# Attention pairs: where v is transposed and rounded, and where q is evacuated

## Chip, cores and metric

The kernel runs on one core of one Trainium2 chip. The metric is device time in microseconds of that core, the median over runs. The numbers are float32; products are made from operands split into a rounded high part and a low remainder (hi·hi + lo·hi + hi·lo), three matmuls for one.

## What is computed

A two-layer encoder trunk on x of 512 tokens by 1024 channels. Layer 0 mixes tokens with a Conformer convolution module, layer 1 with forgetting attention (16 heads of 64, causal, 128-query blocks); each is followed by a squared-ReLU MLP. Only the attention bears on the change:

```python
proj = h @ w_in                       # q, k, v for 16 heads, and the forget logits
F = cumsum(log_sigmoid(f_logit + b_f))
s = q_blk @ k.T * HEAD_DIM**-0.5 + (F_q - F_k)
s = where(kpos <= qpos, s, -1e30)
p = softmax(s)
o = p @ v                             # then o @ w_o
```

## The kernel before

Attention is done in 8 pairs of heads, at about 630 to 860 us of the span. Six pairs are a hardware loop, the seventh has the same code, and the eighth makes no further projection but fills TensorE with products of the output projection. TensorE transposes, makes scores and products; ScalarE makes the rounded high parts and the exponentials; VectorE makes the low parts, masks, normalises and takes the projections out of PSUM; GpSimd writes two operand blocks for the coming pair. Each engine goes through one list, `SEQ`, and does for each entry its own share, in that order; nothing but the order of the list and the semaphores sets what follows what. What the entries mean (i is the index; hh, j = i // 4, i % 4 are head and query block):

- `P` i: TensorE alone, a twelfth of the next pair's projection (six 512-column matmuls). P0 to P3 give q into bank 0, P4 to P7 k into bank 1, P8 to P11 v into bank 2.
- `S` i: TensorE makes scores into bank 4 or 5 (L840, L841), and may do so once the mask of S(i-2) has read that bank. VectorE masks and takes the row's bound (L1964), then normalises block i-1 (`normalise`: reciprocal L1952, scaling L1955) once its exponential is done. ScalarE makes the exponential (L1331).
- `V`: TensorE transposes v of this pair, four blocks (L847), into bank 3. ScalarE rounds it into `vhi` (L1336), VectorE subtracts into `vlo` (L1974).
- `T` i: TensorE transposes probabilities (L875), into bank 6 for even i and bank 3 for odd i, and waits for the low part of T(i-2), which has to leave that bank. ScalarE makes `pThi` (L1354), VectorE `pTlo` (L1991).
- `O` i: TensorE multiplies v by the transposed probabilities of one head into bank 7, `OUTP` (L885 to L887), ScalarE makes `ohi` (L1360), VectorE `olo` (L2001).
- `EVAC` 0, 1, 2: VectorE scales q (`q_evac`, L1883), k (`k_evac`, L1898) and v (`v_evac`, L1910) of the next pair out of PSUM into `tmp`.
- `PARTS` 0, 1: ScalarE rounds q (`q_hi`, two operations, L1282) or k (`k_hi`, L1292); VectorE subtracts (`q_lo`, two, L1890; `k_lo`, two, L1903). `AGAIN`: ScalarE copies of both.
- `SPLIT` i: ScalarE rounds a weight block (L927), VectorE subtracts (L1380).

GpSimd's two operations of a pair (L471) wait for S3 and for S7. In the eighth pair EVAC, PARTS and SPLIT 0 and 1 do nothing. S5's wait is for the mask of S3, T6's for `pTlo` of T4, T7's for that of T5. VectorE and ScalarE take their entries strictly in order: all of VectorE's work between T3 and T4 in the list stands ahead of `pTlo` of T4.

Of the kernel before, what the change touches and what calls it, by code (L numbers as in the profile page):

```python
# [4 lines left out]
F32 = mybir.dt.float32  # L5
F32R = mybir.dt.float32r
ALU = mybir.AluOpType
ACT = mybir.ActivationFunctionType
ds = bass.ds

P = 128
# [52 lines left out]
def raw_slots(c):  # L64

    p = [0, 1, 2, 3]
    for _ in range(c):
# [24 lines left out]

SEQ = [("SPLIT", 2), ("P", 0), ("P", 1), ("S", 0), ("S", 1), ("V", 0), ("P", 2), ("S", 2), ("S", 3),
# [3 lines left out]
       ("T", 7), ("P", 11), ("SPLIT", 1), ("AGAIN", 0), ("AGAIN", 1), ("O", 1), ("EVAC", 2)]  # L97
PARTS_OF_P = 12
# [1 line left out]
def build(nc, x, g_mix_pre, g_mix_post, g_ffn_pre, g_ffn_post, conv_pw1_w, conv_pw1_b, conv_dw_w,  # L100
# [74 lines left out]
    vhi = put("vhi", [P, TB, P], F32R, aa)  # L175
    vlo = put("vlo", [P, TB, P], F32R, aa)
# [14 lines left out]
    tmp = put("tmp", [P, 4, S], F32)  # L191
# [24 lines left out]
    psum = nc.alloc_psum_tensor("psum", [P, 8, 512], F32)  # L216

    STAT, SCORE, TRP, OUTP = 6, 4, (6, 3), 7
# [16 lines left out]
    s = {n: nc.alloc_semaphore(n) for n in sem_names}  # L235
# [6 lines left out]
    def flat(ap):  # L242
        return ap.rearrange("p a b -> p (a b)")
# [35 lines left out]
    with nc.Block() as block:  # L279
# [204 lines left out]
        def _(pe):  # L484
# [342 lines left out]
            def attention(p, project, fill=None):  # L827
                for what, i in SEQ:
                    hh, j = i // 4, i % 4
                    if what == "S":  # L830
                        if i == 0:
                            for name, each in (("q_hi", 4), ("q_ready", 2), ("k_hi", 4), ("k_ready", 2)):
                                pe.wait_ge(s[name], each * p + each)
                        if j == 0:
                            pe.wait_ge(s["f_ready"], 2 * p + (hh + 1))
                        pe.wait_ge(s["sc_evac"], 8 * p + (i + 1))
                        n = P * (j + 1)
                        o = psum[:, SCORE + i % 2, 0:n]
                        qs = slice(j * P, (j + 1) * P)
                        pe.matmul(o, qa[:, hh, qs], ka[:, hh, 0:n], start=True, stop=False)  # L840
                        pe.matmul(o, qb[:, hh, qs], kb_[:, hh, 0:n], start=False,  # L841
                                  stop=True).then_inc(s["sc_done"], 1)
                    if what == "V":
                        pe.wait_ge(s["pr_evac"], 3 * p + 6)
                        pe.wait_ge(s["pt_ready"], 8 * p + 2)
                        for q in range(TB):
                            t = pe.transpose(psum[:, 3, q * P:(q + 1) * P], tmp[:, 2, q * P:(q + 1) * P],  # L847
                                             ident[:, :])
                        t.then_inc(s["vtr"], 1)
                    if what == "P" and fill:  # L850
                        for u, kb in fill[i]:
                            if kb == 0:
                                pe.wait_ge(s["pr_evac"], 3 * PAIRS + u + 1)
                                weights(N_WO, u)
                            if u == 0 and kb == KB - 2:
                                pe.wait_ge(s["o_ready"], 2 * (PAIRS - 2) + 3)
                            product(u, u, kb, ohi[:, kb, :], olo[:, kb, :], kb == 0, False)
                    if what == "P" and project:
                        u, part = i // 4, i % 4
                        n = N_ATT + 1 + p  # L860
                        if part == 0:
                            weights(n, u) if u < 2 else pe.wait_ge(w_ready[1], 2 * n + 2)
                            pe.wait_ge(s["pr_evac"], 3 * p + (3 + u + 1))
                        for kb in (2 * part, 2 * part + 1):
                            mm = product(u, u, kb, hhi[:, kb, :], hlo[:, kb, :], kb == 0, kb == KB - 1)
                        if part == 3:
                            mm.then_inc(unit[u // 2], 2 if u == 2 else 1)
                    if what == "T":
                        pe.wait_ge(s["p_ready"], 8 * p + (i + 1))
                        pe.wait_ge(s["pt_ready"], 8 * p + (i + 1))  # L870
                        if i == 1:
                            pe.wait_ge(s["v_ready"], p + 1)
                        pr = probs(hh, j)
                        for kb in range(j + 1):
                            t = pe.transpose(psum[:, TRP[i % 2], kb * P:(kb + 1) * P], pr[:, kb * P:(kb + 1) * P],  # L875
                                             ident[:, :])
                        t.then_inc(s["t_done"], 1)
                    if what == "O":
                        pe.wait_ge(s["v_ready"], p + 1)
                        pe.wait_ge(s["pt_ready"], 8 * p + (4 * i + 6))  # L880
                        pe.wait_ge(s["o_ready"], 2 * p + (i + 1))
                        for kb in range(TB):
                            o = psum[:, OUTP, kb * P:S]
                            ph, pl = pThi[:, kb, kb * P:S], pTlo[:, kb, kb * P:S]
                            pe.matmul(o, vhi[:, kb, :], ph, start=kb == 0, stop=False)  # L885
                            pe.matmul(o, vhi[:, kb, :], pl, start=False, stop=False)
                            mm = pe.matmul(o, vlo[:, kb, :], ph, start=False, stop=kb == TB - 1)  # L887
                        mm.then_inc(s["pv_done"], 1)
# [30 lines left out]
        def _(act):  # L919
            a = nc.scalar  # L920
# [404 lines left out]
            def attention(p, project):  # L1325
                for what, i in SEQ:
                    hh, j = i // 4, i % 4
                    if what == "S":
                        act.wait_ge(s["sc_evac"], 8 * p + (i + 3))
                        pr = probs(hh, j)  # L1330
                        a.activation(pr, pr, ACT.Exp, scale=-1.0, bias=negmax[:, i:i + 1],  # L1331
                                     accum_out=den[:, i:i + 1]).then_inc(s["ex_done"], 1)
                    if what == "V":
                        act.wait_ge(s["vtr"], p + 1)
                        act.wait_ge(s["pv_done"], 2 * p + 1)
                        a.activation(flat(vhi[:, :, :]), psum[:, 3, :], ACT.Copy).then_inc(s["v_hi"], 1)  # L1336
                    if what == "PARTS" and project:
                        (q_hi, k_hi)[i](p + 1)
                    if what == "AGAIN" and project:
                        (q_again, k_again)[i](p + 1)  # L1340
                    if what == "SPLIT" and project:
                        if i < 2:
                            split_hi(N_ATT + 2 + p, i)
                        else:
                            split_hi(N_ATT + 1 + p, 2, single=True)
                    if what == "SPLIT" and not project and i == 2:
                        split_hi(N_WO, 2)
                        split_hi(N_WO, 3)
                    if what == "T":
                        act.wait_ge(s["t_done"], 8 * p + (i + 9))  # L1350
                        if j == 0:
                            act.wait_ge(s["pv_done"], 2 * p + (hh + 1))
                        src = psum[:, TRP[i % 2], 0:(j + 1) * P].rearrange("p (a b) -> p a b", b=P)
                        a.activation(pThi[:, 0:j + 1, j * P:(j + 1) * P], src,  # L1354
                                     ACT.Copy).then_inc(s["p_hi"], 1)
                    if what == "O":
                        act.wait_ge(s["pv_done"], 2 * p + (i + 2))
                        rows = slice(HD * i, HD * i + HD)
                        dst = ohi[rows, p, :] if isinstance(p, int) else flat(ohi[rows, ds(p, 1), :])
                        a.activation(dst, psum[rows, OUTP, :], ACT.Copy).then_inc(s["o_hi"], 1)  # L1360
# [12 lines left out]
        def _(dve):  # L1373
            d = nc.vector
# [573 lines left out]
            def attention(p, project):  # L1948
# [8 lines left out]
                for what, i in SEQ:  # L1957
                    hh, j = i // 4, i % 4
                    if what == "S":
# [9 lines left out]
                            normalise(i - 1)  # L1969
                        if i == 7:  # L1970
                            normalise(7)
                    if what == "V":
                        dve.wait_ge(s["v_hi"], p + 1)
                        d.tensor_tensor(flat(vlo[:, :, :]), psum[:, 3, :], flat(vhi[:, :, :]).bitcast(F32),  # L1974
                                        ALU.subtract).then_inc(s["v_ready"], 1)
                    if what == "EVAC" and project:
                        (q_evac, k_evac, v_evac)[i](p + 1)
# [97 lines left out]
```

## Time and profile before

| | |
|---|---|
| median of 3 runs | 1240.94 us (1238.62 to 1244.83) |
| the profiled execution: its time, its span | 1244.29 us, 1242.6 us |
| TensorE busy, matmuls | 1189.3 us, 96% |
| VectorE, ScalarE, GpSimd busy | 944.5 us, 664.9 us, 84.3 us |
| mean granted TensorE clock | 0.989 |
| attention's pairs | about 631 to 860 us, one each 28.6 us |

A row of a timeline gives start, duration, engine, line, operation, output<-input, shapes, count, and in brackets the idle time just before it with what ended it. Matmuls overlap: a 512-column matmul is shown with about 0.39 us, and the next starts 0.23 us after it.

### The profile page before, as it was taken

What the parts mean: (1) busy time and instruction counts of PE and PEld (TensorE: products, weight loads), DVE (VectorE), ACT (ScalarE), POOL (GpSimd) and SP (SyncE); (2) the same over time, 40 slices, a digit from 0 to 9 for tenths busy, and PEclk for the clock granted to TensorE, in tenths of its full rate; (3) what the DMA queues carried; (4) which work ended last, traced back from release to release, by engine and by line L of the source; (5) the groups of instructions that cost most, each with busy time, mean ns of one, the idle gap of its engine ahead of it and who ended that gap; (6) DMA issues with size and microseconds to landing.
All of it is one profiled execution on the core that took longest, in us unless ns stands there. A gap on an engine that the chain in (4) does not pass through costs nothing. (4 is left out here: it accounts for less than half of the span.)

```text
span 1242.6 us, 15969 instructions
## 1 busy us (share of the span) xinstructions
PE 1189.3 (96%) x5566; PEld 978.8 (79%) x5566; DVE 944.5 (76%) x1372; ACT 664.9 (54%) x1140; POOL 84.3 (7%) x97
## 2 busy tenths in 40 slices
PE   7999999999999999999879999989999999999996
PEld 6788888878888888887867777768878888888885
DVE  4799986489569579589787777775589579587698
ACT  5766555546444344444666666665456444353453
POOL 1001100040000000004310000000030000000000
PEclk9999999999999999999989999999999999999998
DMA  4312202511520513313021122220510521515301
GB/s 142 102 35 68 68 0 71 170 57 45 170 102 15 189 68 102 135 35 85 18 51 51 51 55 77 66 89 15 189 36 34 189 82 41 192 38 170 102 18 68
DMA packets 103671, 102.25 MB, mean 82 GB/s; under 512 B 4621, under 2 KB 86541, under 8 KB 103610
## 3 DMA queue, kind: packets, MB, share of 16 engines
q1 hardware_dynamic: 103520, 101.27, 25.7%
q8 instruction: 36, 0.59, 0.2%
q10 hardware_dynamic: 90, 0.18, 0.0%
q14 instruction: 25, 0.20, 0.0%
HBM read 99.34 MB, written 2.10 MB: 82 GB/s over the span
## 5 line engine op out<-in xcount | busy, mean ns | idle before, releaser
L493 PE MATMUL psum<-hhi,whi 128*128 128x512 f32 x872 | 348.5, 400 | 6.9 <-DVE hlo L1397 3.7
L495 PE MATMUL psum<-hhi,wlo 128*128 128x512 f32 x872 | 341.6, 392 | 0.0
L494 PE MATMUL psum<-hlo,whi 128*128 128x512 f32 x872 | 341.4, 391 | 0.0
L949 ACT ACTIVATE whi<-mraw 128x1024 fp32r<-128x1024 f32 x176 | 185.4, 1054 | 143.9 <-PE psum L688 111.5
L1391 DVE TENSOR_TENSOR wlo<-mraw,whi 128x1024 fp32r<-128x1024 f32 x176 | 214.0, 1222 | 42.7 <-ACT whi L949 42.6
L493 PEld LDWEIGHTS psum<-hhi,whi 128*128 128x128 f32 x872 | 164.6, 189 | 43.6 <-issue 7.3
L495 PEld LDWEIGHTS psum<-hhi,wlo 128*128 128x128 f32 x872 | 164.4, 189 | 35.1
L494 PEld LDWEIGHTS psum<-hlo,whi 128*128 128x128 f32 x872 | 164.6, 189 | 32.3 <-issue 0.7
L686 PE MATMUL psum<-whi,aop_hi 128*128 128x512 f32 x448 | 175.4, 392 | 0.8 <-DVE wlo L1391 0.8
L688 PE MATMUL psum<-whi,aop_lo 128*128 128x512 f32 x448 | 174.5, 390 | 0.0
L687 PE MATMUL psum<-wlo,aop_hi 128*128 128x512 f32 x448 | 174.4, 389 | 0.0
L1123 ACT ACTIVATE pair<-tmp 128x512 f32<-128x512 f32 x64 | 40.4, 632 | 156.0 <-DVE tmp L1616 156.0
L1616 DVE SCALAR_TENSOR_TENSOR tmp<-psum,rinv 128x512 f32<-128x512 f32 x64 | 44.0, 690 | 77.6 <-PE psum L495 76.2
L686 PEld LDWEIGHTS psum<-whi,aop_hi 128*128 128x128 f32 x448 | 84.1, 188 | 18.3 <-DVE wlo L1391 1.2
L688 PEld LDWEIGHTS psum<-whi,aop_lo 128*128 128x128 f32 x448 | 84.1, 188 | 17.5
L687 PEld LDWEIGHTS psum<-wlo,aop_hi 128*128 128x128 f32 x448 | 84.2, 188 | 17.0
L1670 DVE TENSOR_TENSOR mraw<-mraw 128x1024 f32<-128x1024 f32 x64 | 78.0, 1222 | 2.0 <-DVE wlo L1391 0.5
L1380 DVE TENSOR_TENSOR wlo<-wraw,whi 128x1024 fp32r<-128x1024 f32 x52 | 63.5, 1225 | 7.3 <-ACT whi L927 7.3
L1331 ACT ACTIVATE prob<-prob,negmax 128x128 f32<-128x128 f32 (+1 forms) x64 | 35.9, 561 | 46.0 <-DVE negmax L1964 46.0
L1466 DVE SCALAR_TENSOR_TENSOR y<-upad,vec,y 128x512 f32 (+1 forms) x69 | 54.8, 794 | 0.3
L927 ACT ACTIVATE whi<-wraw 128x1024 fp32r<-128x1024 f32 x52 | 53.7, 1051 | 0.5
L1466 DVE SCALAR_TENSOR_TENSOR acc<-upad,vec,acc 128x512 f32<-128x512 f32 x61 | 46.3, 759 | 0.0
(207 smaller groups left out, 1725.5 us busy)
## 6 DMA issues: line engine op xcount, KB each, us to landing
mraw<-in_mlp_w_up SPq DMA_DIRECT2D x64, 512.0 KB, 4.9
mraw<-in_mlp_w_down SPq DMA_DIRECT2D x64, 512.0 KB, 4.7
wraw<-in_conv_pw_w SPq DMA_DIRECT2D x20, 512.0 KB, 4.5
wraw<-in_attn_w_in SPq DMA_DIRECT2D x16, 512.0 KB, 4.5
wraw<-in_attn_w_in SPq DMA_DIRECT2D x16, 256.0 KB, 3.1
wraw<-in_attn_w_o SPq DMA_DIRECT2D x8, 512.0 KB, 4.1
xin<-in_x SPq DMA_DIRECT2D x4, 512.0 KB, 8.4
wraw<-in_conv_pw_w SPq DMA_DIRECT2D x8, 256.0 KB, 7.6
```

The costliest lines, as they stand in the source:

```text
L493: pe.matmul(o, whi[:, u, kb, :], xhi, start=start, stop=False)
L494: pe.matmul(o, whi[:, u, kb, :], xlo, start=False, stop=False)
L495: return pe.matmul(o, wlo[:, u, kb, :], xhi, start=False, stop=stop)
L686: pe.matmul(o, ah, wh, start=kt == 0 and (not kept or c == 0), stop=False)
L687: pe.matmul(o, ah, wl, start=False, stop=False)
L688: return pe.matmul(o, al, wh, start=False, stop=kt == 3 and (not kept or c == CHUNKS - 1))
L927: a.activation(whi[:, u, :, :], wraw[:, r, :, c * P:(c + 1) * P], ACT.Copy).then_inc(w_hi[r], 2 if single else 1)
L949: a.activation(split_unit(whi, e), raw_unit(c, e_), ACT.Copy).then_inc(s["m_hi"], 1)
L1380: d.tensor_tensor(wlo[:, u, :, :], wraw[:, r, :, c * P:(c + 1) * P], whi[:, u, :, :].bitcast(F32), ALU.subtract).then_inc(w_ready[r], 2 if ...
L1391: d.tensor_tensor(split_unit(wlo, e), raw_unit(c, e_), split_unit(whi, e).bitcast(F32), ALU.subtract).then_inc(s["m_ready"], 1)
L1466: d.scalar_tensor_tensor(dst, upad[:, r, t:t + S], vcol(V_DW + t, j), dst, ALU.mult, ALU.add).then_inc(s["tap"], 1)
L1670: d.tensor_tensor(to, to, mraw[:, p[PLUS[i]], half], ALU.add).then_inc(s["t_sum"], 1)
```

## The change

Only the order of `SEQ`, a bank, and two waits change. TensorE still transposes v after S1, but into bank 7, the bank of the output products, and waits for the previous pair's last `olo` in place of the previous pair's last reads of bank 3. ScalarE and VectorE round v in a new entry `VSPLIT`, after T1, no longer after S1. T1 no longer waits for `vlo`. `EVAC` 0 moves from ahead of T1, and `PARTS` 0 from ahead of T2, to behind T3. The operations and their number are the same.

```diff
-       ("EVAC", 0), ("T", 1), ("PARTS", 0), ("T", 2), ("P", 7), ("T", 3), ("P", 8), ("SPLIT", 0),
+       ("T", 1), ("VSPLIT", 0), ("T", 2), ("P", 7), ("T", 3), ("EVAC", 0), ("PARTS", 0), ("P", 8), ("SPLIT", 0),
        ("EVAC", 1), ("O", 0), ("T", 4), ("P", 9), ("PARTS", 1), ("T", 5), ("T", 6), ("P", 10),
...
-                        pe.wait_ge(s["pt_ready"], 8 * p + 2)
+                        pe.wait_ge(s["o_ready"], 2 * p + 1)
                         for q in range(TB):
-                            t = pe.transpose(psum[:, 3, q * P:(q + 1) * P], tmp[:, 2, q * P:(q + 1) * P],
+                            t = pe.transpose(psum[:, OUTP, q * P:(q + 1) * P], tmp[:, 2, q * P:(q + 1) * P],
                                              ident[:, :])
...
-                        if i == 1:
-                            pe.wait_ge(s["v_ready"], p + 1)
...
-                    if what == "V":
+                    if what == "VSPLIT":
                         act.wait_ge(s["vtr"], p + 1)
                         act.wait_ge(s["pv_done"], 2 * p + 1)
-                        a.activation(flat(vhi[:, :, :]), psum[:, 3, :], ACT.Copy).then_inc(s["v_hi"], 1)
+                        a.activation(flat(vhi[:, :, :]), psum[:, OUTP, :], ACT.Copy).then_inc(s["v_hi"], 1)
...
-                    if what == "V":
+                    if what == "VSPLIT":
                         dve.wait_ge(s["v_hi"], p + 1)
-                        d.tensor_tensor(flat(vlo[:, :, :]), psum[:, 3, :], flat(vhi[:, :, :]).bitcast(F32),
+                        d.tensor_tensor(flat(vlo[:, :, :]), psum[:, OUTP, :], flat(vhi[:, :, :]).bitcast(F32),
                                         ALU.subtract).then_inc(s["v_ready"], 1)
```

## Rows read from the trace of the kernel before

**Rows 1.** Windows, a whole pair: us, busy of each engine, PEclk, DMA, GB/s

```profile
689.00:718.00 29.00, 27.24 (x140) 21.87 (x139) 21.96 (x54) 18.12 (x39) 2.07 (x2) 1.00 0.22 59
```

**Rows 2.** Waits of TensorE, 660 to 833 us: us in total, times, longest

```profile
PE psum L875 <- DVE pTlo L1991: 5.5, 11, 0.8
PE psum L840 <- DVE negmax L1964: 3.8, 6, 0.7
```

**Rows 3.** Timeline of TensorE, third pair: S2, S5, T3, T5, T6, T7

```profile
691.75 0.34 PE L841 MATMUL psum<-kb,qb 128*128 128x384 f32 x1
...
694.83 0.39 PE L840 MATMUL psum<-ka,qa 128*128 128x256 f32 x1 [0.65 <-DVE negmax L1964]
...
703.15 0.60 PE L875 MATMUL psum<-ident,prob 128*128 128x128 f32 x4
...
708.80 0.38 PE L875 MATMUL psum<-ident,prob 128*128 128x128 f32 x2
709.33 0.52 PE L875 MATMUL psum<-ident,prob 128*128 128x128 f32 x3 [0.16 <-DVE pTlo L1991]
...
711.11 0.63 PE L875 MATMUL psum<-ident,prob 128*128 128x128 f32 x4
```

**Rows 4.** Timeline of VectorE, the same pair

```profile
692.53 0.69 DVE L1974 TENSOR_TENSOR vlo<-psum,vhi 128x512 fp32r<-128x512 f32 x1 [0.63 <-ACT vhi L1336]
693.13 0.55 DVE L1964 CUSTOM_DVE_ANT_0 prob<-psum,causal 128x384 f32<-128x384 f32 x1
...
693.80 0.35 DVE L1955 TENSOR_SCALAR prob<-prob,rden 128x256 f32<-128x256 f32 x1
694.08 0.69 DVE L1964 CUSTOM_DVE_ANT_0 prob<-psum,causal 128x512 f32<-128x512 f32 x1
...
697.95 0.93 DVE L1955 TENSOR_SCALAR prob<-prob,rden 128x256 f32<-128x256 f32 x1
...
701.17 0.68 DVE L1883 SCALAR_TENSOR_TENSOR tmp<-psum,rinv 128x512 f32<-128x512 f32 x1
...
702.63 1.41 DVE L1890 TENSOR_TENSOR qa<-tmp,qa 64x512 fp32r<-64x512 f32 x2 [0.45 <-ACT qa L1282]
...
705.49 1.23 DVE L1380 TENSOR_TENSOR wlo<-wraw,whi 128x1024 fp32r<-128x1024 f32 x1 [0.27 <-ACT whi L927]
706.64 0.69 DVE L1898 TENSOR_TENSOR tmp<-psum,rinv 128x512 f32<-128x512 f32 x1
708.31 0.68 DVE L2001 TENSOR_TENSOR olo<-psum,ohi 64x512 f32 x1 [0.98 <-ACT ohi L1360]
708.91 0.27 DVE L1991 TENSOR_TENSOR pTlo<-psum,pThi 128x128 fp32r<-128x128 f32 x1
...
712.40 0.69 DVE L1991 TENSOR_TENSOR pTlo<-psum,pThi 128x512 fp32r<-128x512 f32 x1 [0.98 <-ACT pThi L1354]
```

**Rows 5.** Timeline of ScalarE, the same pair

```profile
701.97 1.28 ACT L1282 ACTIVATE qa<-tmp 64x512 fp32r<-64x512 f32 x2 [0.91 <-DVE tmp L1883]
...
704.40 1.06 ACT L927 ACTIVATE whi<-wraw 128x1024 fp32r<-128x1024 f32 x1
```

**Rows 6.** Timeline of GpSimd, the same pair

```profile
692.75 1.04 POOL L471 TENSOR_TENSOR qb<-gates_q,onehot 64x512 fp32r<-64x512 f32 x1 [22.64 <-PE psum L841]
697.69 1.03 POOL L471 TENSOR_TENSOR qb<-gates_q,onehot 64x512 fp32r<-64x512 f32 x1 [3.91 <-PE psum L841]
```

**Rows 7.** Timeline of TensorE, eighth pair: S4 and S5

```profile
837.73 0.30 PE L840 MATMUL psum<-ka,qa 128*128 128x128 f32 x1 [1.16 <-DVE negmax L1964]
...
838.71 0.39 PE L840 MATMUL psum<-ka,qa 128*128 128x256 f32 x1 [0.57 <-DVE negmax L1964]
```

**Rows 8.** Timeline of TensorE outside attention, two lone waits

```profile
43.38 0.50 PE L607 MATMUL psum<-uhi,diaghi 128*128 128x512 f32 x1 [1.83 <-DVE ulo L1495]
...
915.60 0.50 PE L493 MATMUL psum<-hhi,whi 128*128 128x512 f32 x1 [1.38 <-DVE hlo L1397]
```

**Rows 9.** Windows, TensorE alone: us, busy, PEclk, DMA, GB/s

```profile
43.00:48.00 5.00, 4.62 (x13) 0.66 0.00 2
838.00:843.00 5.00, 4.43 (x15) 0.66 0.18 62
914.00:919.00 5.00, 3.62 (x19) 1.00 0.00 0
```

## The prediction

> **What bounds the kernel now.** I read the page first. TensorE is busy nearly all of the span, so any work moved between other engines counts only where TensorE waits for it. Then the windows, one for each pair of heads: in a steady pair TensorE is busy 27.24 of 29 us at full clock, VectorE only 21.96 and ScalarE 18.12 [rows 1]. VectorE has room on average; the question is where its queue is late. The table of waits over six pairs names two places: scores wait for a mask, six times 0.63 us (S5, once a pair), and transposes wait for a low part, eleven times, 5.5 us in all (T2, and a little at T6) [rows 2]. Last the timelines of the third pair, engine by engine, to follow who stands in whose queue [rows 3 to 6]. Pairs repeat to 0.1 us, so what holds for this one is multiplied. The end of the span is far behind attention and follows it: time won or lost on TensorE in a pair reaches the end.
>
> **First part: v's rounding leaves the mask queue.** `vlo` costs VectorE 0.63 us of waiting for `vhi` and about 0.60 us of work (692.53 to 693.13) directly ahead of the mask of S2 [rows 4]. Without it that mask can start when S2 is ready. S2's last matmul starts at 691.75 and lasts 0.34 [rows 3], so the mask starts at 692.1 to 692.3 and not at 693.13. If all behind it moved along, the mask of S3, on which S5 waits, would come about 0.85 us earlier, and S5's wait (0.65 us shown, somewhat more with the restart of the weight load) would be gone.
>
> I do not think that it moves along. Behind the mask of S2 stands the scaling of block 1, 0.67 us after the mask's start (693.13 to 693.80) [rows 4]: it would now come at 692.8 to 693.0. GpSimd runs its first operation from 692.75 to 693.79, released by S3, whose time on TensorE does not change [rows 6]. Before, the scaling started just after that end and took 0.35 us. The second operation of GpSimd, from 697.69 to 698.72, shows what happens when the same scaling, same shape, starts inside it: 697.95, and 0.93 us long, to 0.16 us past GpSimd's end [rows 4, 6]. So the scaling of block 1 will now take some 0.95 us, the mask of S3 starts at 693.79 + 0.08 = 693.87 where it was 694.08 (back to back, the next operation starts 0.07 to 0.08 ahead of the shown end), and S5 gains 0.21 us, not 0.75. Bounds: 0 and 0.8 us; I take 0.21, since the two patterns have the same spacing.
>
> The Trainium skill states this as a rule (SBUF — State Buffer, Who interferes with whom): VectorE in a two-port mode and GpSimd take a shared port pair in turn, exclusively, and the one that issues first keeps it for its whole instruction. The trace agrees for the second operation; by the rule the first part of the change gives 0.21 us, without it 0.8.
>
> From S5 on everything shifts by that much: T2 waits for `pTlo` of T0, which stands behind masks and exponentials that shift with the scores. T1's dropped wait on `vlo` was long fulfilled: nothing. TensorE's new wait at V is for `olo` of the previous pair, which VectorE finishes ahead of `v_evac`, on which V waits anyhow: nothing. Bank 7 is empty between O1 and O0: nothing. `vhi` and `vlo` behind T1 take ScalarE and VectorE 0.6 us each where `q_evac`, `q_hi` and `q_lo` stood (701.17 to 704.04 on VectorE), so `pTlo` of T2 and T3 is, if anything, earlier; T3 still has its bank in time.
>
> **Second part: q's evacuation behind T3.** Here is the loss. VectorE's queue between T3 and T4 was: `wlo`, `k_evac`, `olo`. It gains `q_evac` and two `q_lo` at its head, and ScalarE's gains two `q_hi` ahead of its weight rounding. The queues depend on each other, so the chain is walked, from T3's start on TensorE to T6's, which waits for `pTlo` of T4:
> - T3 to the start of its `pTlo`: as for T7, also of four blocks, 711.11 to 712.40: 1.29 [rows 3, 4]
> - that `pTlo`, start to start: 0.60, as 708.31 to 708.91 [rows 4]
> - `q_evac` to first `q_hi`, 701.17 to 701.97: 0.80 [rows 4, 5]
> - two `q_hi`: 1.28 [rows 5]. The two `q_lo` beside them end sooner (0.66 + 1.41 = 2.07 after the first `q_hi`) than what follows
> - weight rounding on ScalarE to `wlo`, 704.40 to 705.49: 1.09 [rows 4, 5]
> - `wlo`, 705.49 to 706.64: 1.15 [rows 4]
> - `k_evac` 0.60 and `olo` 0.60, now back to back. The 0.98 us of waiting ahead of `olo` is the only cover there was, and it is used up
> - `pTlo` of T4 to T6, 708.91 to 709.33: 0.42 [rows 3, 4]
>
> Together 7.83 us, where T3 to T6 took 709.33 - 703.15 = 6.18 [rows 3]. T6 is late by 1.65, less the 0.21 won: 1.44 us a pair. T7 can't come sooner behind T6 than now (1.78) [rows 3]; `k_hi` and `k_lo` are pushed back by the same chain and end at about the time T7 wants them, so they add 0 to 0.1. Nothing later in the pair gives it back: P10, P11, O1 follow in order, and the next pair's q is needed only at its S0. Seven pairs project: 7 x 1.44 = 10.1 us.
>
> **The eighth pair** has no EVAC, PARTS or GpSimd work. There S4 waits 1.16 us and S5 0.57 us for masks [rows 7], and the removed wait and work of `vlo` (0.63 + 0.60) stood ahead of both. S4's wait goes: 1.16. These waits were also followed by a fall of the granted clock, mean 0.66 over 838 to 843 us, that is 5 x 0.34 = 1.7 us of full-speed time [rows 9]; with half the waiting it should stay up, but S7 then meets its mask, so I count half. Together -2.0 us (bounds -1.2 and -2.9).
>
> **The clock in the seven pairs.** T5 ends at 709.18 now and at 708.97 or a little sooner after; T6 starts at 709.33 + 1.44 = 710.77. TensorE will stand still for 1.8 to 2.0 us in each of seven pairs. A lone wait of 1.83 us at 43.38 was followed by half clock: 43 to 48 us has a mean of 0.66, and 1.7 us is lost beyond the wait; a lone wait of 1.38 us at 915.60 was not: 1.00 [rows 8, 9]. The new wait is nearer the first, but just at its size. Bounds: none of seven falls, or all, at up to 1.7 us each. I take four, at 1.5 us (a part of each falls where TensorE has slack ahead of O1): 6.0 us.
>
> **Sum.** 10.1 - 2.0 + 6.0 = +14.1 us. On the profiled execution: 1244.29 + 14.1 = 1258.4 us (span 1242.6 + 14.1 = 1256.7). That execution lies 3.4 us above the median of the runs; the forecast for a median is 1240.94 + 14.1 = 1255 us, 1.1% slower. A measurement of this kernel tells about 0.5%, 6.2 us, from no change.
>
> **Rivals.**
> - The forecast, wait at T6 with the clock falling in some of the pairs: chance 0.60, 1251 to 1262.
> - The wait at T6, but the clock stays up, as after the 1.38 us wait: 10.1 - 2.0 = +8.1, 1249 us. For it: the wait could be 1.8 or less. Chance 0.20.
> - The port: the scaling starts ahead of GpSimd's operation and holds the pair of ports itself. Then S5 wins 0.75 and not 0.21 in seven pairs, 3.8 us less: 1245 us without falls of the clock, 1251 with. Against it: 0.1 to 0.2 us of margin in GpSimd's favour. By the skill's page (same section, issue order decides) this is the case where the scaling gets there first. Chance 0.10; split between same and slower.
> - The other side: q's evacuation is hidden. It would be if T3 to T6 took less than 6.18 us with `q_evac`, `q_hi`, `q_lo` in the queue: VectorE would have to run `q_lo` and `wlo` while waiting, with the weight rounding on ScalarE not behind `q_hi`. Then only the gains stay: 6 x 0.21 to 0.75, and 2.0: -3.3 to -6.5, 1234 to 1238 us. It decides at 1.65 us less than my chain; the list's order speaks against it. Chance 0.06.
> - A change that moves little because the moved work finds other cover: 1238 to 1246 us, 0.04.
>
> Faster 0.05, same 0.10, slower 0.85. The range goes from the low end of the rival of the port to all clocks fallen (10.1 - 1.2 + 11.9 = +20.8): 1245 to 1262.
>
> **What would show it.** In the trace after: no `vlo` between the masks; the scaling of block 1 at about 0.9 us inside GpSimd's first operation, and S5 still waiting 0.4 to 0.6 us; on VectorE `q_evac` right behind `pTlo` of T3, `olo` directly behind `k_evac`; T3 to T6 7.8 us; TensorE idle 1.8 to 2.0 us ahead of T6 seven times, a pair of 30.1 us at full clock, more where the clock falls; the eighth pair shorter. The prediction is wrong if ScalarE's weight rounding starts ahead of `q_hi`, if the scaling keeps 0.35 us, or if the clock falls nowhere or always.

## The result, and the profile after

| | before | after |
|---|---|---|
| median | 1241.95 us (4 runs, 1238.62 to 1244.83) | 1255.46 us (4 runs, 1254.18 to 1257.77) |
| ratio | | 1.0116, 95% interval 1.0098 to 1.0135 |
| profiled execution: time, span | 1244.29, 1242.6 us | 1254.18, 1252.4 us |

The kernel became 13.5 us slower by the medians; 1255 was forecast. The profiled executions differ by 9.9 us: the one before lies 2.3 us above its median, the one after 1.3 us below. Between 640 and 876 us TensorE's waits after are these, in us in total, times, longest:

```profile
PE psum L873 <- DVE pTlo L1989: 19.0, 14, 1.9
PE psum L840 <- DVE negmax L1962: 4.8, 9, 0.8
```

The same two waits as in [rows 2], but that for the low part has grown: over the same stretch it was 6.5 us in 13 waits before, none above 0.8 us. The third pair on TensorE, S5, T2, T3, T5, T6, T7, O1 (lines are two lower than before):

```profile
697.92 0.38 PE L840 MATMUL psum<-ka,qa 128*128 128x256 f32 x1 [0.49 <-DVE negmax L1962]
...
704.50 0.52 PE L873 MATMUL psum<-ident,prob 128*128 128x128 f32 x3 [0.80 <-DVE pTlo L1989]
706.25 0.60 PE L873 MATMUL psum<-ident,prob 128*128 128x128 f32 x4
...
711.76 0.38 PE L873 MATMUL psum<-ident,prob 128*128 128x128 f32 x2
714.08 0.52 PE L873 MATMUL psum<-ident,prob 128*128 128x128 f32 x3 [1.94 <-DVE pTlo L1989]
715.86 0.63 PE L873 MATMUL psum<-ident,prob 128*128 128x128 f32 x4
717.90 0.50 PE L883 MATMUL psum<-pThi,vhi 128*128 128x512 f32 x1
```

T6 stands idle for 1.94 us where it was 0.16 [rows 3]. T3 to T6 is 714.08 - 706.25 = 7.83 us, the walked sum to the hundredth. VectorE, the masks of S2 and S3 with the scaling between them, then the queue behind T3:

```profile
695.62 0.56 DVE L1962 CUSTOM_DVE_ANT_0 prob<-psum,causal 128x384 f32<-128x384 f32 x1 [0.41 <-PE psum L841]
...
696.30 0.96 DVE L1953 TENSOR_SCALAR prob<-prob,rden 128x256 f32<-128x256 f32 x1
697.18 0.68 DVE L1962 CUSTOM_DVE_ANT_0 prob<-psum,causal 128x512 f32<-128x512 f32 x1
...
707.52 0.69 DVE L1989 TENSOR_TENSOR pTlo<-psum,pThi 128x512 fp32r<-128x512 f32 x1 [1.38 <-ACT pThi L1352]
708.12 0.68 DVE L1881 SCALAR_TENSOR_TENSOR tmp<-psum,rinv 128x512 f32<-128x512 f32 x1
709.59 1.40 DVE L1888 TENSOR_TENSOR qa<-tmp,qa 64x512 fp32r<-64x512 f32 x2 [0.78 <-ACT qa L1280]
711.33 1.23 DVE L1378 TENSOR_TENSOR wlo<-wraw,whi 128x1024 fp32r<-128x1024 f32 x1 [0.34 <-ACT whi L925]
712.47 0.68 DVE L1896 TENSOR_TENSOR tmp<-psum,rinv 128x512 f32<-128x512 f32 x1
713.07 0.67 DVE L1999 TENSOR_TENSOR olo<-psum,ohi 64x512 f32 x1
713.67 0.27 DVE L1989 TENSOR_TENSOR pTlo<-psum,pThi 128x128 fp32r<-128x128 f32 x1
```

ScalarE, the two steps between, and GpSimd's first operation of the pair:

```profile
708.92 1.29 ACT L1280 ACTIVATE qa<-tmp 64x512 fp32r<-64x512 f32 x2 [1.44 <-DVE tmp L1881]
710.23 1.06 ACT L925 ACTIVATE whi<-wraw 128x1024 fp32r<-128x1024 f32 x1
```

```profile
696.07 1.04 POOL L471 TENSOR_TENSOR qb<-gates_q,onehot 64x512 fp32r<-64x512 f32 x1 [24.29 <-PE psum L841]
```

To be seen: the mask of S2 waits for TensorE now, as it should; the scaling behind it starts 0.23 us into GpSimd's operation and takes 0.96 us, to 697.26, 0.15 us past its end. And behind T3: `olo` follows `k_evac` with no idle time, where [rows 4] had 0.98 us.

The granted clock fell behind the waits of the fourth and sixth pair (columns as in [rows 9]):

```profile
744.00:748.00 4.00, 3.86 (x14) 0.57 0.00 0
806.00:810.00 4.00, 4.00 (x15) 0.58 0.00 0
```

Lengths of pairs, from one O1's start to the next: 30.05, 30.06, 31.59, 30.07, 31.58, 30.03 after, 28.39 to 28.67 before; the eighth 27.03, where it was 29.16. In the eighth pair S4 waits no more, and S7 does, as expected:

```profile
850.13 0.30 PE L840 MATMUL psum<-ka,qa 128*128 128x128 f32 x1
...
851.11 0.39 PE L840 MATMUL psum<-ka,qa 128*128 128x256 f32 x1 [0.57 <-DVE negmax L1962]
...
853.01 0.50 PE L840 MATMUL psum<-ka,qa 128*128 128x512 f32 x1 [0.35 <-DVE negmax L1962]
```

The balance of the two profiled spans: -0.3 us up to the first scores, +2.2 in the first pair, +11.8 in the next six (8.7 of it the wait, 3.1 two falls of the clock), -2.1 in the eighth, -1.7 behind attention: +9.9. Nothing that the change touches runs behind attention. From the last O1 to the end, three of the thirteen profiles have 385.9 us (the kernel before is one of them) and ten 384.2 to 384.4 us, for which no run shows a cause.

Of the -2.1 us in the eighth pair, a part is not there in every execution. The profile before has a fall of the clock there, at 839.1 us. Two other profiles (q's part alone, and the kernel before with GpSimd moved) leave v's rounding where it was, have no fall there, and take 28.38 us for this pair. Against those the changed kernel wins 1.35 us.

### The profile page after: what moved, and what is told of

Same layout as the page of the kernel before. It is cut to its first block and busy times, and to the rows that moved or that the text cites. A ratio compares the mean times of both kernels' runs of the same rounds, so it can differ in the third digit from the quotient of the medians.

```text
span 1252.4 us, 15969 instructions
## 1 busy us (share of the span) xinstructions
PE 1188.3 (95%) x5566; PEld 978.8 (78%) x5566; DVE 946.4 (76%) x1372; ACT 664.4 (53%) x1140; POOL 85.0 (7%) x97
## 5 line engine op out<-in xcount | busy, mean ns | idle before, releaser
L1989 DVE TENSOR_TENSOR pTlo<-psum,pThi 128x128 fp32r<-128x128 f32 (+1 forms) x64 | 29.9, 485 | 25.0 <-ACT pThi L1352 24.7
```

## The experiments

Ratios are to the kernel before on the same chip, with the 95% interval. Pair lengths are from the profile, O1 to O1, at full clock.

| run | ratio | interval | a pair, us | falls of the clock in seven pairs |
|---|---|---|---|---|
| changed kernel | 1.0116 | 1.0098 to 1.0135 | 30.05 | 2 |
| v's part alone | 0.9976 | 0.9966 to 0.9985 | 28.6 | 0 |
| q's part alone | 1.0108 | 1.0091 to 1.0125 | 30.3 | 3 |
| changed, 12 matmuls in the wait | 1.0093 | 1.0078 to 1.0108 | 30.6 | 0 |
| changed, GpSimd at T3 and O0 | 1.0095 | 1.0078 to 1.0113 | 29.5 | 6 |
| v's part, GpSimd at T3 and O0 | 0.994 | 0.9923 to 0.9957 | 27.6 | 0 |
| before, GpSimd at T3 and O0 | 0.9975 | 0.9962 to 0.9988 | 28.1 | 0 |
| changed, GpSimd at T3 | 1.0095 | 1.0076 to 1.0115 | 28.9 | 4 |
| changed, 8 matmuls in the wait | 1.0077 | 1.0062 to 1.0092 | 30.1 | 0 |
| v's part, GpSimd, q's split behind T3 | 0.9923 | 0.9909 to 0.9938 | 27.5 | 0 |
| changed, weight split ahead of q's | 1.0003 | 0.9989 to 1.0017 | 29.0 | 0 |
| changed kernel again | 1.0094 | 1.0077 to 1.011 | 30.05 | 2 |

**v's part alone.** q's evacuation and split back where they were:

```diff
-       ("T", 1), ("VSPLIT", 0), ("T", 2), ("P", 7), ("T", 3), ("EVAC", 0), ("PARTS", 0), ("P", 8), ("SPLIT", 0),
+       ("EVAC", 0), ("T", 1), ("VSPLIT", 0), ("PARTS", 0), ("T", 2), ("P", 7), ("T", 3), ("P", 8), ("SPLIT", 0),
```

> Of the change only v's part: v transposed into bank 7, rounded behind T1; q's evacuation and split stay where they were (EVAC 0 ahead of T1, PARTS 0 behind the rounding of v). My theory (the loss is q's chain between T3 and T4; v's part gains a little): T6 waits 0.2 us or less, the scaling of block 1 takes about 0.95 us inside GpSimd's operation, S5 still waits 0.4 to 0.5 us, a pair is 28.4 us where it was 28.6, the eighth pair 2 us shorter: 3 to 4 us faster than before, ratio 0.997. Rival, that v's rounding between T1 and T2 is what delays VectorE's queue ahead of T4: T6 waits over 1 us here too and the kernel is 8 us or more slower.

1240.63 against 1243.4 us: 2.8 us faster, where 3 to 4 were expected. T6 waits 0.17 us, so v's place has no part in the loss. But the pair did not get shorter, 28.6 us: what S5 wins O0 gives back.

```profile
693.32 0.39 PE L840 MATMUL psum<-ka,qa 128*128 128x256 f32 x1 [0.49 <-DVE negmax L1962]
...
704.03 0.47 PE L883 MATMUL psum<-pThi,vhi 128*128 128x512 f32 x1 [0.37 <-issue]
...
708.04 0.52 PE L873 MATMUL psum<-ident,prob 128*128 128x128 f32 x3 [0.17 <-DVE pTlo L1989]
```

`vlo` stands ahead of `q_lo` in VectorE's queue, and `pTlo` of T3 behind it. That this is what O0 waits for is not shown by the row, which names no releaser; the last experiment bears it out. By the pairs the gain is in the eighth alone, 27.05 us where it was 28.38 without a fall of the clock and 29.16 with one.

**q's part alone.** v in bank 3 and rounded after S1 as before:

```diff
-       ("EVAC", 0), ("T", 1), ("PARTS", 0), ("T", 2), ("P", 7), ("T", 3), ("P", 8), ("SPLIT", 0),
+       ("T", 1), ("T", 2), ("P", 7), ("T", 3), ("EVAC", 0), ("PARTS", 0), ("P", 8), ("SPLIT", 0),
```

> Of the change only q's part: v is transposed into bank 3 and rounded after S1 as before; EVAC 0 and PARTS 0 stand behind T3. My theory: T3 to T6 7.8 us where it was 6.2, a pair 1.6 us longer than before, the eighth pair as before, the clock falling behind some of the seven waits at T6 (two did in the changed kernel): 11.5 us, and 1.5 for each fall, so 12 to 17 us slower than before, and 2 to 4 us slower than the changed kernel. Rival, that both parts are needed for the loss: under 5 us slower than before.

1256.86 against 1243.4, 13.5 us slower. T3 to T6 is 7.84 us:

```profile
709.20 0.60 PE L875 MATMUL psum<-ident,prob 128*128 128x128 f32 x4
...
717.04 0.52 PE L875 MATMUL psum<-ident,prob 128*128 128x128 f32 x3 [1.95 <-DVE pTlo L1991]
```

A pair without a fall is 30.3 us, 1.66 more than before, against 1.65 walked. This part makes the whole loss; the changed kernel's difference to it (0.2 us a pair and 1.35 us in the eighth) is v's part. I expected 2 to 4 us between the two; by the times they can't be told apart.

**The weight block's split ahead of q's.** One swap in the changed kernel's list (the part of the line that changes), the same operations between T3 and T4:

```diff
-("T", 3), ("EVAC", 0), ("PARTS", 0), ("P", 8), ("SPLIT", 0),
+("T", 3), ("EVAC", 0), ("P", 8), ("SPLIT", 0), ("PARTS", 0),
```

> The changed kernel with one swap in the list: the weight block's split (SPLIT 0) ahead of q's (PARTS 0), q's evacuation first as in the change. The work between T3 and T4 is the same, only VectorE no longer stands waiting for q_hi and for the rounding. If the loss is the walked chain with its waits for ScalarE: 1.29 + 0.60 + 0.60 + 1.15 + 1.41 + 0.60 + 0.60 + 0.42 = 6.7 us from T3 to T6 and not 7.8, T6 waits 0.7 us, no fall of the clock, a pair of 28.9 us: 0 to 1 us slower than before, 12 us faster than the changed kernel. If the loss were the mere amount of work of q on VectorE there: T3 to T6 over 7.5 us still, 8 us slower than before or more.

1243.57 against 1243.49: the loss is gone from the time of the kernel.

```profile
701.58 0.60 PE L873 MATMUL psum<-ident,prob 128*128 128x128 f32 x4
...
708.35 0.52 PE L873 MATMUL psum<-ident,prob 128*128 128x128 f32 x3 [0.87 <-DVE pTlo L1989]
```

```profile
703.45 0.68 DVE L1881 SCALAR_TENSOR_TENSOR tmp<-psum,rinv 128x512 f32<-128x512 f32 x1
704.05 1.21 DVE L1378 TENSOR_TENSOR wlo<-wraw,whi 128x1024 fp32r<-128x1024 f32 x1
705.30 1.40 DVE L1888 TENSOR_TENSOR qa<-tmp,qa 64x512 fp32r<-64x512 f32 x2
706.73 0.69 DVE L1896 TENSOR_TENSOR tmp<-psum,rinv 128x512 f32<-128x512 f32 x1
```

```profile
702.71 1.05 ACT L925 ACTIVATE whi<-wraw 128x1024 fp32r<-128x1024 f32 x1
```

T3 to T6 is 6.77 us (6.7 walked). VectorE does the same work without a gap: ScalarE rounds the weights from 702.71 to 703.76, while VectorE makes T3's low part and begins to evacuate q. Of the 1.65 us, 1.06 was waiting across engines; the 0.59 that is left I put down to VectorE's work for q. The profile shows no fall behind these waits of 0.87 us. A pair is still 29.0 us, 0.4 more than before; the shorter eighth pair makes up for it.

**Small matmuls in the wait.** Ahead of T6, in the seven projecting pairs, 12 or 8 matmuls of ones into a score bank that nobody reads; they add work and change no output:

```diff
+                    if what == "T" and i == 6 and project:
+                        pe.wait_ge(s["sc_evac"], 8 * p + 9)
+                        keep_warm(12, bank=SCORE)
```

> The changed kernel with 12 small matmuls on a bank that nobody reads, ahead of T6 in the seven projecting pairs, 1.7 us of TensorE work inside its 1.9 us wait. If the waits cost only their own length and the clock falls behind some of them: T6 starts where it did behind T3 (7.8 us), the granted clock is 1.00 in every pair from the second on, and the time is 1.5 us less for each fall that the changed kernel has, 3 to 6 us less than it. If the clock's falls come from elsewhere: as many falls as without, and the same time.

> The changed kernel with 8 small matmuls ahead of T6, where 12 took 2.7 us and pushed T6 back by 0.6 us. Eight take 1.8 us, so T6 starts where it does without them and TensorE stands idle 0.3 to 0.4 us. No fall of the clock in the seven pairs, a pair of 30.05 us every time: what is left of the loss is the wait alone, 7 x 1.44 - 2.1 = 8 us slower than before, ratio 1.0065; and the changed kernel's other 4 to 5 us are the clock's falls. Rival, that the changed kernel's excess is not the clock: 1.010 or more with the clock at full.

> The changed kernel itself, once more, for the share of the clock: with 8 small matmuls in the wait it was 1.0077 of before with the clock at full in all seven pairs. If the clock's falls are the rest, this one is at 1.010 to 1.013, its profile shows two to four falls behind the waits at T6, and pairs are 30.05 us without a fall and 31.6 with one. If it is at 1.008 or less, the small matmuls saved nothing.

Twelve were too many: one takes 0.22 us, all 2.7, and the pair grew by 0.55 us. Even so the kernel was not slower. Eight fit, and T6 starts 7.83 us behind T3:

```profile
705.50 0.60 PE L877 MATMUL psum<-ident,prob 128*128 128x128 f32 x4
...
711.24 1.95 PE L505 MATMUL psum<-ones 128*128 128x128 f32 x16
713.33 0.52 PE L877 MATMUL psum<-ident,prob 128*128 128x128 f32 x3
```

(A row of these counts two for one matmul.) The clock is 1.00 throughout 640 to 844 us:

```profile
640.00:844.00 204.00, 193.86 (x1036) 1.00 0.19 54
```

1250.6 against 1241.26, 9.3 us slower, 1.0077. The changed kernel again is 1255.83 against 1243.49, 12.3 us slower, with falls behind the third and fifth wait. The two intervals overlap (1.0062 to 1.0092, 1.0077 to 1.011), so by the times the clock's share is about 3 us and could be 0 to 5; by the traces it is two falls of 1.5 us.

The mean granted clock of each execution, profiled or not, says the same. It is 0.987 over ten executions of the changed kernel, 0.990 over 51 of the kernel before, and 0.991 over the six with eight small matmuls. Among the 51, a clock lower by 0.001 goes with 1.1 us more time. The changed kernel's clock is lower by 0.0028, which makes about 3 us (an estimate from these numbers).

**GpSimd released later.** In the changed kernel, in v's part alone, and in the kernel before, GpSimd's first operation waits for T3 and the second for O0's end:

```diff
-                for hh in range(2):
-                    pool.wait_ge(s["sc_done"], 8 * p + (4 * hh - 4))
-                    head_rows(2 * p + hh, hh)
+                pool.wait_ge(s["t_done"], 8 * p + 4)
+                head_rows(2 * p, 0)
+                pool.wait_ge(s["pv_done"], 2 * p)
+                head_rows(2 * p + 1, 1)
```

> The changed kernel with GpSimd's two operations for the next pair released later: the first by T3, the second by O0's end, in place of S3 and S7. If GpSimd's operations hold up the scalings of blocks 1 and 5: both take 0.35 us, S5 waits 0.1 us or less and T2 0.2 to 0.3 us where it waited 0.8, T3 comes 1.0 to 1.3 us sooner after S0, and as T3 to T6 stays 7.8 us, the kernel is 7 to 9 us faster than the changed kernel. If the scaling is slow there for another reason: 0.9 us still, and no change of time.

Half right. The scaling is free, 0.35 us, S5 starts 0.36 us behind S4 (700.16 and 699.80) with no wait shown, T3 comes 12.58 us behind S0 where it was 13.65. Yet the time, 1256.0 against 1243.4, is that of the changed kernel, where 7 to 9 us less were expected. VectorE, TensorE and GpSimd:

```profile
699.02 0.35 DVE L1954 TENSOR_SCALAR prob<-prob,rden 128x256 f32<-128x256 f32 x1
...
712.99 1.65 DVE L1379 TENSOR_TENSOR wlo<-wraw,whi 128x1024 fp32r<-128x1024 f32 x1 [0.34 <-ACT whi L926]
```

```profile
716.18 0.52 PE L874 MATMUL psum<-ident,prob 128*128 128x128 f32 x3 [2.37 <-DVE pTlo L1990]
```

```profile
712.24 1.31 POOL L471 TENSOR_TENSOR qb<-gates_q,onehot 64x512 fp32r<-64x512 f32 x1 [2.50 <-PE psum L886]
```

The second operation now lies on `wlo`, which has two operands in SBUF, and holds it up by 0.42 us (1.65 us in all seven pairs, 1.22 elsewhere), on the very chain that T6 waits for. The wait grew to 2.37 us and the clock fell in six of seven pairs; such a pair takes 30.7 us and not 29.5. What was won was given back by a collision that the move itself made. With both released by T3, where the VectorE operations beside them (`pTlo` of T3, `q_evac`) have one tensor in SBUF or none:

```diff
+                pool.wait_ge(s["t_done"], 8 * p + 4)
                 for hh in range(2):
-                    pool.wait_ge(s["sc_done"], 8 * p + (4 * hh - 4))
                     head_rows(2 * p + hh, hh)
```

> The changed kernel with both of GpSimd's operations released by T3, where VectorE has only operations with one operand in SBUF. In the run that released the second by O0's end it lay on the weight block's subtraction, which took 1.65 us and not 1.23, T3 to T6 took 8.3 us, TensorE's wait was 2.4 us and the clock fell in six of seven pairs. Here the subtraction takes 1.23 us, T3 to T6 7.8, the wait is 1.9 us, T3 still comes 1.07 us sooner: 7 us faster than the changed kernel with as many falls of the clock (two or three), 4 us faster with two more. Rival, that the clock falls as often as in that run although the wait is 1.9 us: no more than 2 us faster than the changed kernel.

`wlo` takes 1.23 us, T6 waits 1.90, a pair without a fall is 28.9 us, 1.1 less than in the changed kernel; the profiled span is 1247.8, 4.6 us less. The clock fell in four pairs. The median is 1252.27 against 1241.26, 11.0 us slower than before: 1.3 to 2.5 us less than the changed kernel was slower, where 4 were expected with this many falls. That is also what the rival allowed, no more than 2 us, and the ratio is that of the changed kernel run again. The pairs bear the mechanism out (1.1 us shorter at full clock), the times don't resolve it.

In the version without q's part, and in the kernel before:

> Only v's part of the change, and GpSimd's two operations released later: the first by T3, the second by the end of O0. In the run with v's part alone the pair was as long as before: S5's wait and T2's wait of 0.8 us stayed, and O0 gave back what S5 won. In the run with GpSimd moved in the changed kernel both waits went and T3 came 1.07 us sooner after S0. If the two are additive: S5 waits 0.1 us or less, T2 0.25, both scalings take 0.35 us, T6 waits 0.2 or less as before, a pair is 27.6 us, the eighth pair 27.0: 9 us faster than before, ratio 0.993. Rival, that the time won goes into a longer wait at O0 or T6: under 4 us faster.

> The kernel before with nothing but GpSimd's two operations moved, as in the run beside it. v is still rounded between the masks of S1 and S2, so S5's wait stays at 0.65 us; only the scaling of block 5 is set free, and T2 waits 0.25 us where it waited 0.8. 0.5 us a pair, 3 to 4 us faster than before, ratio 0.997. If this gives the whole 7 us or more, v's place in the queue has no part in it; if nothing, GpSimd's hold only matters once v is out of the queue.

1233.66 against 1241.26, 7.6 us faster (9 expected), and 1238.63, 2.6 us faster (3 to 4 expected). The waits of the first of the two:

```profile
PE psum L884 <- issue: 2.9, 7, 0.6
PE psum L874 <- DVE pTlo L1990: 2.6, 13, 0.3
PE psum L841 <- DVE negmax L1963: 1.8, 3, 0.9
```

The two edits are not a plain sum. In a steady pair v's part alone gives 0, GpSimd alone 0.54 us, both 1.05: v's place pays in these pairs only once GpSimd is out of the masks' way. O0's 0.4 us stayed, so I moved q's split, and only that, behind T3:

```diff
-       ("EVAC", 0), ("T", 1), ("VSPLIT", 0), ("PARTS", 0), ("T", 2), ("P", 7), ("T", 3), ("P", 8), ("SPLIT", 0),
+       ("EVAC", 0), ("T", 1), ("VSPLIT", 0), ("T", 2), ("P", 7), ("T", 3), ("PARTS", 0), ("P", 8), ("SPLIT", 0),
```

> The version with v's part and GpSimd moved (a pair of 27.57 us, O0 waiting 0.4 us), and q's split (PARTS 0) moved behind T3, q's evacuation staying ahead of T1. Walking the queue as in the prediction: pTlo of T3 comes 1.29 us behind T3 and no longer 1.7, so O0 wins 0.3 us; behind it q_lo, then the weight block's subtraction, which waits for ScalarE (two q_hi and the rounding: 1.26 + 1.28 + 1.09 = 3.6 us behind T3), then 1.15 + 0.6 to olo at 5.4 to 5.5 us behind T3, where O0 allows it at 5.1: T6 0.3 to 0.4 us later behind T3. The two cancel: a pair of 27.6 us, within 1.5 us of the version without the move, ratio 0.993. If the whole of q's chain were harmful wherever it stands: T6 waits over 1 us and the pair is 28.5 us.

1234.73 against 1243.49, 8.8 us faster, the lowest ratio: 0.9923. It can't be told from the one without the move. Its pair is 0.1 us shorter: O0 no longer waits, as expected once `vlo` and `q_lo` no longer both stand ahead of `pTlo` of T3, and T6 waits 0.37 us where it was 0.17.

## Why the prediction was right

- **S5 gains 0.21 us.** Right in size and cause. The scaling took 0.96 us inside GpSimd's operation (0.95 forecast), and releasing GpSimd later restored 0.35. Between 640 and 850 us of the kernel before, the scaling of 128x256 took 0.94 us each of the 7 times that it met GpSimd and 0.35 us each of the 8 times that it did not; `vlo`, with one tensor in SBUF, took 0.69 us either way. The rule of the Trainium skill (SBUF — State Buffer, Who interferes with whom), an exclusive port pair kept by the one that issues first, agrees: the scaling ended 0.15 us past GpSimd's end. The same section has an instruction with two SBUF inputs contend with a GpSimd instruction that reads SBUF. `wlo` is one, and it ended 1.09 us past GpSimd's end, where it takes 1.22 alone.
- **`pTlo` of T3 not later, T3 in time, V and T1 free.** Right for the changed kernel: T3 comes 13.65 us behind S0 where it was 13.86, and O0 2.06 behind T3 where it was 2.18. With q ahead of T3, `vlo` in the same place makes that 2.36.
- **T3 to T6 7.83 us.** Measured 7.83, with steps of 1.27, 0.60, 0.80, 1.31, 1.10, 1.14, 0.60, 0.60, 0.41. 1.44 us a pair: measured 30.06 against 28.62. q's part alone and the swap of the two splits show that this chain is the loss.
- **The eighth pair -2.0 us.** Measured -2.1 between the two profiles. S7 met its mask, the clock stayed up. But the fall that it took half of is not in every execution of the kernel before, and without it the pair wins 1.35 us.
- **The clock, 6.0 us.** Right that it falls behind waits of 1.9 us, and 1.5 us for one fall (31.6 against 30.05). The count, "I take four", was mis-sized: two in each of two profiles of the changed kernel, so 3.1 us, and about 3 us by the mean clock of all executions. The first pair lost 0.8 us more than the 1.44; in it the clock came back up later, with a mean over 634 to 636 us of 0.67 where it was 0.92, behind a wait for the first scores that both kernels have.
- **The sum.** +14.1 forecast; +9.9 between the profiled executions, +13.5 and +12.3 by the medians of two comparisons. That 1255 was met so closely is in part luck: the medians agree with the forecast better than its terms deserve. The terms as measured give 10.1 + 3.1 - 2.1 = 11.1 us, or 11.9 with 1.35 for the eighth pair. The 0.4 to 2.4 us that the medians have beyond this are open. Between the two profiles 11.1 becomes 9.9 by what lies outside the terms: -0.3 ahead of the first scores, +0.8 in the first pair, -1.7 behind attention. And falls of the clock outside the pairs differ between executions: one at 193 to 195 us is in ten of the thirteen profiles, in the one before and not in the one after.

## What to carry to other kernels

When an operation is moved in in-order queues, walk the chain step by step through every engine, with start-to-start times of rows, instead of comparing totals: VectorE had 7 us to spare in each pair and still became the wait, mostly by standing idle for ScalarE. Put between a producer and its consumer on the other engine something that needs neither; one swap of that kind gave back 1.06 us of 1.44 a pair and, by the profile, the falls of the clock, which was enough to bring the kernel back to its old time. And when GpSimd and VectorE overlap, look at which VectorE operations read two tensors in SBUF, or read and write SBUF alone at a high rate (the scaling takes 0.49 us for 128x512, the mask out of PSUM 0.68). A later release was worth 2.6 us alone and 7.6 us together with v's part (2.8 alone), and where it landed on the wrong operation it was worth nothing.

## What was unexpected

- Waits of 1.83 to 1.95 us at T6 were followed by half clock in 11 of 28 cases (2, 2, 3 and 4 of 7, in four profiles), waits of 2.28 to 2.38 us in 6 of 7, of 0.87 us in none of 7. The lone wait of 1.83 us at 43 us [rows 8], which the prediction read in one profile, is in all thirteen and was followed by a fall in six. So the same wait can pass or cost 1.5 us more, and its length alone does not decide; what else does is not shown. Seven cases are few to say that 0.4 us of added waiting brings more falls.
- A GpSimd operation of 1.04 us lengthens VectorE's scaling from 0.35 to 0.96 us, and a subtraction with two SBUF operands from 1.23 to 1.65. It is itself lengthened, to 1.30 or 1.31 us in all seven cases, where it starts inside another such subtraction (`q_lo` runs to 712.65, GpSimd starts at 712.24).
